# A two-block transformer layer: opening operands in three groups, the experts' second block requested in the routing phase, and one block's up products placed ahead of the other block's down products

## The reference

```
def expert_block(args):
    xblk, e = args
    return (jax.nn.silu(xblk @ w1[e]) * (xblk @ w3[e])) @ w2[e]
yb = lax.map(expert_block, (xb, block_expert)).reshape(n_rows, u.shape[1])
y = yb[dest] * sw[:, None].astype(u.dtype)
```

## Time and profile before

| | |
|---|---|
| device time, median of 3 runs (lowest to highest) | 4396.33 us (4392.52 to 4397.52) |
| the profiled execution's own time | 4396.28 us |
| its span, first to last instruction | 4394.5 us |
| PE busy | 3982.7 us (91%) |
| DVE, ACT, POOL busy | 1482.2, 1014.7, 605.7 us |
| HBM read, written | 514.20 MB, 71.05 MB |
| first experts phase, from PE's first to last product | 1581.5 to 2231 us |
| second experts phase | 4021.7 to 4347 us |

### The profile page before, as it was taken

The page is one execution under the profiler, slowest core; times in us unless marked ns, Lnnn a source line. Parts: engine busy times, 40 slices in busy tenths (PEclk is TensorE's granted clock), DMA queues, the critical chain, the costliest instruction groups (busy, mean ns, idle before and its releaser), DMA issues. The chain is left out here.

```text
span 4394.5 us, 95415 instructions
## 1 busy us (share of the span) xinstructions
PE 3982.7 (91%) x41485; PEld 2613.4 (59%) x41485; DVE 1482.2 (34%) x2542; ACT 1014.7 (23%) x2416; POOL 605.7 (14%) x732
## 2 busy tenths in 40 slices
PE   7798999998999969999978999989999989997995
PEld 2343446885444458888854444469888944445774
DVE  2555412133121320000042666655566532222003
ACT  2200110032010112222243442034444311112333
POOL 1030000001100000000010001334454311000112
PEclk8899999999999979999989999989999999997997
DMA  6362302003112079999971001100000031124998
GB/s 214 117 200 81 129 24 72 29 10 66 38 37 93 34 286 390 391 396 398 396 250 28 10 2 43 43 2 4 4 3 4 4 97 43 58 84 183 392 388 316
DMA packets 233424, 588.67 MB, mean 134 GB/s; under 512 B 36456, under 2 KB 140807, under 8 KB 213224
## 3 DMA queue, kind: packets, MB, share of 16 engines
q1 hardware_dynamic: 192447, 462.92, 28.9%
q0 software_dynamic: 19120, 73.68, 4.9%
q10 hardware_dynamic: 21626, 48.70, 3.2%
HBM read 514.20 MB, written 71.05 MB: 133 GB/s over the span
## 5 line engine op out<-in xcount | busy, mean ns | idle before, releaser
L1650 PE MATMUL experts_bank<-experts_uT,ex_wu 128*64 128x96 f32 x9216 | 391.5, 247 | 27.0 <-PE experts_bank L1636 21.3
L1650 PEld LDWEIGHTS experts_bank<-experts_uT,ex_wu 128*64 128x64 f32 x9216 | 385.1, 138 | 43.7 <-issue 43.7
L1723 DVE TENSOR_TENSOR experts_hT<-experts_si,experts_bank 128x384 f32<-128x384 f32 (+1 forms) x68 | 31.3, 460 | 723.1 <-PE experts_bank L1650 723.1
L192 PE MATMUL vgproj_bank<-vg_w,mix_hT 128*128 128x256 f32 x1024 | 225.7, 383 | 11.1 <-DVEq L201 7.7
L192 PEld LDWEIGHTS vgproj_bank<-vg_w,mix_hT 128*128 128x128 f32 x1024 | 195.7, 192 | 41.5 <-DVEq L201 8.5
L1650 PE MATMUL experts_bank<-experts_uT,b2z_hT 128*64 128x96 f32 x4096 | 177.7, 248 | 25.3 <-DMA b2z_hT<-in_w 12.7
L1650 PEld LDWEIGHTS experts_bank<-experts_uT,b2z_hT 128*64 128x64 f32 x4096 | 172.2, 138 | 40.0 <-issue 40.0
L1636 PE MATMUL experts_bank<-mixed_T,experts_hT 128*32 128x256 f32 (+1 forms) x2592 | 193.9, 451 | 0.0
L2247 POOL TENSOR_TENSOR b2z_hT<-b2z_hT,rwkv_level 128x256 f32<-128x256 f32 x192 | 153.8, 833 | 159.3 <-DVE b2z_hT L2600 159.2
L2616 DVE TENSOR_TENSOR rc_xy<-rc_xy,rc_bank 128x256 f32<-128x256 f32 x288 | 120.6, 420 | 122.3 <-PE rc_bank L2261 116.4
L1636 PEld LDWEIGHTS experts_bank<-mixed_T,experts_hT 128*32 128x32 f32 x2592 | 110.4, 110 | 69.6
(11 more groups left out here) (576 smaller groups left out, 7195.4 us busy)
## 6 DMA issues: line engine op xcount, KB each, us to landing
ex_wu<-in_expert_w SPq DMA_DIRECT2D x72, 2048.0 KB
mixed_T<-in_expert_w SPq DMA_DIRECT2D x36, 2048.0 KB, 23.0
b2z_hT<-in_w SPq DMA_DIRECT2D x64, 1024.0 KB
b2z_Z<-in_w SPq DMA_DIRECT2D x32, 1024.0 KB, 12.4
keep_rows<-mix_hyT ACTq DMA_DIRECT2D x27, 768.0 KB
keep_rows<-experts_yo ACTq DMA_DIRECT2D x68, 288.0 KB
mix_hT<-in_ada_w POOLq DMA_DIRECT2D x8, 2048.0 KB, 9.9
merge_w<-in_w_in SPq DMA_DIRECT2D x32, 512.0 KB, 6.1
```

Source lines behind the costliest of these rows:

```text
L192: last = pe.matmul(bk[t][:, 0:width], xT[:, k, t * P:(t + 1) * P], wt[:, s, k, :], start=(k == 0), stop=(k == KT - 1))
L1650: last = pe.matmul(bk[2 + j][c:c + 64, h * BT:(h + 1) * BT], wu[:, s, j, k, h * P + c:h * P + c + 64], uT[:, s, k, :], start=(k == 0), sto ...
```

## The change

Three edits. In the opening, the loads on ACT's queue are counted in three groups: `fed` (`feats`, `w1`), `layered` (three vectors, `w2`) and `spread` (`w3`, `negt`, `delta`), and each user waits for its own; the last seven of the 23 vectors are issued from ACT's queue between `layered` and `spread`, and POOL issues no slice of `ada_w` before `layered` has landed. In routing, SP requests the weights of blocks 0 and 1, not of block 0 alone. In the experts phases PE makes the up products of block n+1 ahead of the down products of block n, `hT` gets two buffers, ACT or DVE frees `wd` in place of PE, and SP's loop requests `wu`, `wu`, `wd`, `wd` for two blocks.

```diff
         @b.gpsimd
         def _(gp):
...
+            gp.wait_ge(layered, 64)
             for n in range(ADA):
...
-            pe.wait_ge(come, 16 * 9)
+            pe.wait_ge(fed, 32)
...
+            for to, what in ((feats[:, :], I["k_feats"]), (w1[:, :], I["hy_ffn_w1"][0])):
+                act.dma_start(to, what).then_inc(fed, 16)
...
+            act.wait_ge(zeroed, 1)
+            for name, n in vectors[SPLIT:]:
+                act.dma_start(*row_of(name, n)).then_inc(loaded, 16)
...
-            dve.wait_ge(come, 16 * 9)
+            dve.wait_ge(layered, 64)
...
-            e = sp.value_load(T.be[0:1, 0:1], min_val=0, max_val=NE - 1)
+            for n in range(2):
+                e = sp.value_load(T.be[0:1, n:n + 1], min_val=0, max_val=NE - 1)
...
             with sp.Fori(0, n1) as i:
-                for s in (1, 0):
-                    e = sp.value_load(T.be[0:1, bass.ds(i * 2 + (2 - s), 1)], min_val=0, max_val=NE - 1)
-                    load(s, e, i * 2 + (3 - s))
+                ups(0, expert(bass.ds(i * 2 + 2, 1)), i * 2 + 3)
+                ups(1, expert(bass.ds(i * 2 + 3, 1)), i * 2 + 4)
+                downs(0, expert(bass.ds(i * 2 + 2, 1)), i * 2 + 3)
+                downs(1, expert(bass.ds(i * 2 + 3, 1)), i * 2 + 4)
...
+            ups(0, 0)
+            with pe.Fori(0, n1) as i:
+                ups(i, 1)
+                downs(i, 0)
+                ups(i, 2)
+                downs(i, 1)
+            ups(n1, 1)
+            downs(n1, 0)
+            downs(n1, 1)
```

More of the change, by code:

```diff
@@ L693, in _ @@
             pe.wait_ge(sine, 1)
+            pe.wait_ge(layered, 64)
             for x in range(2):
@@ L717, in _ @@
         def _(act):
[L718 to L722, removed]
+            for to, what in ((feats[:, :], I["k_feats"]), (w1[:, :], I["hy_ffn_w1"][0])):
+                act.dma_start(to, what).then_inc(fed, 16)
+            for to, what in ((vecs[:, 0:1], I["hy_ffn_b1"].rearrange("a p -> p a")), (vecs[:, 1:2], I["hy_ffn_freq"].rearrange("a p -> p a")),
+                             (vecs[:, 2:3], I["hy_ffn_b2"].rearrange("a p -> p a")), (w2[:, :], I["hy_ffn_w2"][0])):
+                act.dma_start(to, what).then_inc(layered, 16)
+            act.wait_ge(zeroed, 1)
+            for name, n in vectors[SPLIT:]:
+                act.dma_start(*row_of(name, n)).then_inc(loaded, 16)
+            for to, what in ((w3[:, :], I["hy_ffn_w3"][0]), (negt[:, :], I["k_negt"]), (delta[:, :], I["k_delta"])):
+                act.dma_start(to, what).then_inc(spread, 16)
             act.dma_start(brow[:, :], I["ada_b"]).then_inc(browed, 16)
@@ new lines, in downs @@
+            def downs(i, n):
+                s = n % 2
+                pe.wait_ge(gated, i * 2 + (n + 2))
+                pe.wait_ge(wdfull[s], i * 16 + (16 * (n // 2) + 16))
+                pe.wait_ge(yout, i * 4 + (2 * n + 2))
+                for j in range(2):
+                    width = HALF if j == 0 else 256
+                    rest = [(t, k) for t in ((0, 1) if j == 0 else (2,)) for k in range(HT)]
+                    for k in range(HT):
+                        for c in range(3):
+                            last = quarter(s, j, c, c, k, j * HALF, width, 0)
+                        for t, q in rest[k * len(rest) // HT:(k + 1) * len(rest) // HT]:
+                            last = quarter(s, j, 3, t, q, WIDE, 256, t % 2 * 256)
+                    last.then_inc(ymm, 1)
@@ L1639, in _ @@
             pe.wait_ge(xfull[0], 16)
             turn(0)
[L1641 to L1670, removed]
@@ L1703, in _ @@
+            rise(0, 0)
+            with act.Fori(0, n1) as i:
+                rise(i, 1)
+                store(i, 0)
+                rise(i, 2)
+                store(i, 1)
+            rise(n1, 1)
+            store(n1, 0)
+            store(n1, 1)
             for s in range(2):
-                hold(act, saved[s], n * 32 + 32)
+                hold(act, saved[s], n1 * 32 + 64)
         @b.vector
         def _(dve):
-            n = dve.value_load(T.nb[0:1, 0:1], **pairs)
+            n1 = rest_of(dve)
```

132 lines of the change are left out of this document (85 added, 47 removed).

## The result

The changed kernel takes 4535.26 us (median of 4 runs, 4524.94 to 4543.22), the kernel before 4396.93: a ratio of 1.0318 with an interval of 1.0301 to 1.0334. It is 138 us slower. The direction was forecast; the size, +70, was half of it, and the time lies 7 us above the stated range of 4400 to 4528.

What follows compares the result with a forecast made beforehand. PE was taken to set the first experts phase's pace, DMA right behind and beginning to take over in the second. Opening -11, first experts +45, second +36 gave +70 on 4396.28: 4466 us, range 4400 to 4528.

Steps and rivals of the forecast that it cites:

- PE's order and its self-wait: Experts phases: dropping PE's wait for its own last down product gains nothing, DMA hides it, except -1 us per phase.
- Requests come late: Experts phases: SP's new order asks slot 0's `wu` late, once a pair; +30 us in the first, +21 in the second.
- The clock: Experts phases: half the pauses of 2.6 to 2.7 us lower PE's clock, 1.6 us each; +13 and +11 us.
- rival (a): Experts phases: every pause costs the clock and weights land near the upper bound; +137 us there, 4528 in all; chance 0.15.
- The head: Barrier before each experts phase: block 1's early request delays block 0's gather; +3 us first, +5 second.
- -1 each: First pair of each experts phase: its weights are there, so dropping the self-wait gains 1 us each.
- The opening: Kernel's start: small loads land earlier with `ada_w` held back, PE's line 695 at 18 us, not 29.30; -11 us.
- (b): Experts phases: the DMA queue never runs dry, so only its pace counts; pairs of 36.0 and 20.3, 4400; chance 0.15.
- (c): Experts phases: weights land within 17.2 and 9.3 us, PE runs at its own pace; -34 us, 4362; chance 0.10.
- (d): Whole kernel: the experts phases don't move and the opening alone counts; 4385 us; chance 0.05.

Runs made afterwards that it cites:

- mended kernel: Changed kernel with SP's loop requests in the order PE frees buffers, and block 1's `wd` requested in the loop, not in routing: 4382.67 us, ratio 0.9965.
- filled pause: Changed kernel with 40 added PE products, alternating between the bank's halves, ahead of the wait for slot 0's `wu`: 4490.16 us, ratio 1.0212.

## Why the prediction was right and wrong

**PE's order and its self-wait: "DMA hides it". Wrong, by about 10 us, but not where it decides the sum.** I took 394 GB/s for the transfers' own bound; it was the rate that PE's pace asked for. Without the self-wait DMA moves 402 GB/s and the first phase gains 11.6 us, against nothing (or -1 for the first pair) forecast. Where the prediction had 35.9 us as the least for a pair, pairs of 35.0 were measured.

**"Requests come late": right in mechanism, place and count; its size was 0.7 us short of a pair in the first phase.** Forecast from the end of the down products to the landing 20.3 us, measured on average 21.0 (16 x 0.7 = 11 us in all); second phase 12.3 and 13.5 (14 x 1.2 = 17). One piece that the prediction left out is SP's own code: between the second `wd` (ends 1717.81) and `wu` (1719.26) lie a branch and a register load, 1.45 us, where block 0's three requests had followed at once. The mended kernel shows that the order of SP's queue is the whole cause of the loss in the experts phases. What I argued only for PE's new order holds for the old one as well; that came out by an expectation that failed. By the formula of the Trainium skill, "DMA: Bandwidth & Descriptors", section "Anatomy of one DMA", which is fitted there to single DMAs issued by GpSimd, the weights would have landed in time (by the estimates in the prediction after 16.4 and 9.2 us). For these three DMAs of SP with other transfers beside them the trace decides against it, with 21.0 and 13.5.

**The clock: the step that failed.** The prediction said "A pause of 2.6 to 2.7 is close to the point where it turns, so I count half of them", at 1.6 us each, 0.8 a pair. The pauses were 3.9 us in the first phase and 4.3 in the second on average, because of the later landing and because I had counted 0.4 to 0.5 us of branch and self-wait among the work that covers it, while in the changed kernel's rows one set of products follows the other without a gap. In the first phase every pause cost the clock, and 2.5 us of PE on average (1.3 to 2.8), not 1.6 in every second one. In the sum: first phase 16 x (2.5 - 0.8) = 27 us, with the 11 above 38; 42 + 38 = 80, against the 83 measured, and the first pair, below, has 1.4 of the rest. Second phase: work behind the landing 11.0 us in place of 9.3, 14 x (1.7 - 0.8) = 13, with the 17 above 30; 31 + 30 = 61, and 4 us for the first pair, against 63.9. Four of the second phase's pauses, of 2.85 to 2.95 us, were nearly as short as I had thought: three cost 1.7 us each, one nothing, so half was too little even for pauses of that length.

The filled pause shows that the clock is the cause in the first phase; in the second it is what the rows of PE say, and the filled kernel gained little there. The Trainium skill, "TensorE: Matmul & The Clock Gate", Part 1, has half rate as the default, which activity releases; the trace agrees, with a granted clock of 0.50 behind the pause of 3.79 us. I had written that the loss grows if pauses are longer than I think, and gave that case, rival (a), 0.15. It is the one that came near, at 4528. Its pair of 40.6 us in the first phase is as measured, but by luck: it has 0.8 us too much for the landing (21.8 for 21.0) and 0.9 too little for the clock. In the second phase it has 24.2 for 24.4.

**The head.** "+3 and +5 us", measured +6.8 and +2.1 over the routing phases; the sum of 8 is near by luck, since the split is wrong. Of the 6.8, 4.7 is the idle time at the barrier; the rest is about what single traces differ by (without this edit the phase takes 167.9 to 170.3 us). The gather took 12.1 us where I had an upper bound of 11.0. "-1 each" for the first pair was wrong in sign: from the phase's first product to the up products of block 2 it was +0.4 and +3.1 us, when the down products that now come later are counted in. With two sets of up products behind each other, the second stands right behind its own turn and waits for ACT to write `uT`, 3.01 and 2.3 us. Work that lay between a product and its user had been a cover.

**The opening: right.** Second layer at 18 forecast, at 15.1 measured; the gain of 11 was 9.3 to the routing phase in the profiled execution and 12 to 15 in the time of the kernel with the opening alone. The prediction had put the gain on the held-back `ada_w` and the groups together; each half alone gives two thirds of it or more.

**The rivals.** (b), a DMA queue that never runs dry, is what the mended kernel has; the changed one ran dry once in a pair, as argued. (c), weights in time, needed 17 us for 6.3 MB; 21.0 were measured. (d) is refuted by the stage table.

## What to carry to other kernels

When PE's order of releases changes, write the requests in one queue in exactly that order: a wait in front of a request for one buffer is a wait for every request behind it, and two requests of a kind put side by side turn a steady stream into bursts. Read a rate in a saturated phase as what was asked for, not as what can be had, unless the consumer is seen to wait. And when you forecast a stall of PE of a few us, price the clock with it and look how near the stall is to a costlier row; here the clock was half of the first phase's loss.

## What the runs showed of the hardware

- What a pause cost PE, from the up or down products behind it: 2.71 us of pause, 1.7 us; 2.85 to 2.95 us, 1.7 in three cases and nothing in a fourth; 3.71 us, 1.3 us; 3.79 us, 2.8 us, with a granted clock of 0.50 for 5.5 us; 4.88 us, 2.9 us; 5.12 us, 1.7 us. The length of a pause alone didn't tell its price.
- PE's work that nobody uses can pay: 3.5 us of added products in each pair made the changed kernel 45 us faster.
- 80 products into one half of a bank took 13.33 us, 0.17 each; 40 that took turns at its two halves took 3.52, 0.09 each.
- In both experts phases DMA reads as 1.02 busy at 394 and at 402 GB/s (first) and at 384 and 388 (second): in the first the share alone didn't tell that there was room.
